# Prompt attention: the threshold search of the long query tiles counts with sign sums on ScalarE, the products for the maxima stand on both sides of the values' products, and the normalisation is done in an earlier slot

## The reference

```python
def indexer_scores(qi, wi, ki, q_pos, k_pos):
    dots = jnp.einsum('bqhd,bsd->bqhs', qi, ki)            # 8 index heads of 64
    s = jnp.einsum('bqhs,bqh->bqs', jax.nn.relu(dots), wi * IDX_SCALE)
    return jnp.where(k_pos[None, None, :] <= q_pos[None, :, None], s, -jnp.inf)
...
    sc = indexer_scores(qib, wib, ki, q_pos, k_pos)
    _, idx = lax.top_k(sc, 256)                             # 256 keys per query
    valid = idx <= q_pos[None, :, None]
    return sparse_attend(qb, gather_rows(k, idx), gather_rows(v, idx), valid)
...
    s = jnp.where(valid[:, :, None, None, :], s, -jnp.inf)  # 16 heads, 4 kv heads of 64
    p = jax.nn.softmax(s, axis=-1)
    o = jnp.einsum('bqngk,bqknd->bqngd', p, v_sel)
```

## Time and profile before

| | |
|---|---|
| median of 3 runs | 6835.29 us (6826.99 to 6841.92) |
| the profiled execution | 6842.18 us |
| its span in the trace | 6840.6 us |
| stretch of the prompt's attention | about 675 to 3090 us of the span |
| busy in that stretch | PE 1783, DVE 1651, ACT 609, POOL 215 us |

### The profile page before, as it was taken

The page is one execution under the profiler, slowest core; times in us unless marked ns, Lnnn a source line. Parts: engine busy times, 40 slices in busy tenths (PEclk is TensorE's granted clock), DMA queues, the critical chain, the costliest instruction groups (busy, mean ns, idle before and its releaser), DMA issues. The chain is left out here.

```text
span 6840.6 us, 60119 instructions
## 1 busy us (share of the span) xinstructions
PE 4944.6 (72%) x16356; PEld 2498.3 (37%) x16408; DVE 2880.7 (42%) x5354; ACT 1429.0 (21%) x2686; POOL 693.7 (10%) x924
## 2 busy tenths in 40 slices
PE   7998466666779888773647569980888887469970
PEld 2443122222223333332113434430665656344430
DVE  1111657778777666630631321104444443331114
ACT  0111212222222223220012212221222322112212
POOL 0112110000000000110022201002000000101012
PEclk9999678888899999985768579995989897579995
DMA  6111000000000000001433477756001000346865
GB/s 232 49 56 60 17 16 11 11 11 7 11 11 8 8 11 18 10 19 25 153 112 117 143 281 275 276 215 216 23 18 37 18 31 11 98 145 248 299 226 175
DMA packets 194804, 634.25 MB, mean 93 GB/s; under 512 B 47033, under 2 KB 65851, under 8 KB 176044
## 3 DMA queue, kind: packets, MB, share of 16 engines
q1 hardware_dynamic: 130318, 412.71, 17.4%
q0 software_dynamic: 38496, 127.70, 5.7%
q10 hardware_dynamic: 25824, 91.88, 3.3%
HBM read 497.48 MB, written 134.79 MB: 92 GB/s over the span
## 5 line engine op out<-in xcount | busy, mean ns | idle before, releaser
L1966 PE MATMUL experts_ps_gu<-w_sb,experts_xT 128*128 x1504 | 681.6, 607 | 36.1 <-DMA w_sb<-moe_w_in 31.7
L815 DVE TENSOR_SCALAR_CACHE_REDUCE attend_passed<-attend_score,attend_cand 128x512 bf16<-128x512 f32 (+13 forms) x448 | 662.6, 1479 | 47.9 <-issue 4.6
L911 PE MATMUL attend_po<-attend_PT,V 128*128 128x512 f32 x1088 | 544.3, 623 | 12.3 <-ACT attend_total L713 12.3
L2475 PE MATMUL recurrent_psAB<-recurrent_hT,rec_w_in_sb 128*128 128x256 f32 (+1 forms) x2304 | 535.0, 392 | 10.6 <-ACT recurrent_hT L2270 10.6
L703 ACT ACTIVATE attend_PT<-attend_big 128x512 f32<-128x512 f32 x544 | 295.4, 595 | 1051.8 <-PE attend_big L900 1051.3
L469 PE MATMUL project_pj<-project_w,project_hT 128*128 128x512 f32 (+2 forms) x1360 | 507.6, 530 | 6.6 <-ACT project_proj L385 5.5
L2475 PEld LDWEIGHTS recurrent_psAB<-recurrent_hT,rec_w_in_sb 128*128 128x128 f32 x2304 | 463.0, 215 | 76.5 <-issue 11.7
L775 DVE TENSOR_REDUCE attend_mx<-attend_aux 128x1 f32<-128x512 f32 (+3 forms) x640 | 365.6, 607 | 187.1 <-PE attend_aux L922 176.2
L1966 PEld LDWEIGHTS experts_ps_gu<-w_sb,experts_xT 128*128 128x128 f32 x1504 | 285.8, 195 | 366.8 <-issue 366.8
L922 PE MATMUL attend_aux<-attend_KTb,attend_qTb 128*128 128x512 bf16 (+3 forms) x640 | 245.2, 388 | 180.9 <-issue 176.6
L933 PE MATMUL attend_aux<-attend_w_out,attend_oT 128*128 128x512 f32 x512 | 258.7, 669 | 155.4 <-DVE attend_oT L789 155.4
(11 more groups left out here) (378 smaller groups left out, 5966.2 us busy)
## 6 DMA issues: line engine op xcount, KB each, us to landing
w_sb<-moe_w_in SPq DMA_DIRECT2D x64, 2048.0 KB, 11.4
w_sb<-moe_w_in SPq DMA_DIRECT2D x64, 1024.0 KB, 8.3
yb_scratch<-experts_y ACTq DMA_DIRECT2D x94, 512.0 KB, 8.2
index_slab<-ada_w_in SPq DMA_DIRECT2D x12, 2048.0 KB, 7.9
sample_V<-cache_v_in POOLq DMA_DIRECT2D x128, 128.0 KB, 2.6
sample_K<-cache_k_in SPq DMA_DIRECT2D x128, 128.0 KB
route_x<-xa_scratch SPq DMA_DIRECT2D x32, 512.0 KB, 4.7
hs_scratch<-route_h ACTq DMA_DIRECT2D x32, 512.0 KB
```

Of the source, the lines that this page charges most:

```text
L815: dve.tensor_scalar(passed[:, 0:L[m]], score[:, m % 2, 0:L[m]], bound, 0.0, op, ALU.add, accum_out=count[:, :])
L911: pe.matmul(po[:, n % 2, :], V1[:, b, n, :], PT[:, g % 4, :], start=(b == 0), stop=(b == S[i] // NKV - 1)).then_inc(pv_done, 1)
L1966: last = pe.matmul(ps_gu[:, u, :], xT[:, u, k, :], w1[:, bass.ds(slot, 1), k, :].rearrange("p a n -> p (a n)"), start=(k == 0), stop=(k == ...
L2475: last = pe.matmul(psAB[:, c % 2, part, 0:W], w_in[:, k, part * D + c * P:part * D + (c + 1) * P], hT[:, k, 0:W], start=(k == 0), stop=(k ...
```

## The change

Four things change, all in `phase_attend`:

1. For the nine tiles with L of at least 1024 (m = 4 to 12, searched in steps 2 to 10), the counts of rounds 1 to 31 are made by ACT: `weigh` sums sign(score + threshold) over the row into `balance`. DVE still makes the count of round 0, asks for the next sum (`asked`), waits for it (`balanced`) and sets the bit. The value in `cand` is kept negated for this.
2. Round 32 of these tiles first works out the threshold from the negated value: ten operations on one column and one more count over the row. Then `finish_search` follows as before.
3. PE does the first half of a slot's `fill`s ahead of `with_values` and the rest behind, in all steps.
4. `normalise` stands in slot 1 (or slot 0 where a step has no other) instead of the middle slot, in all steps.

```diff
+        def by_act(m):
+            return L[m] >= 1024
+        def asked_of(m):
+            return 31 * sum(by_act(k) for k in range(m))
...
+                def weigh(m, r):
+                    act.wait_ge(asked, asked_of(m) + r + 1)
+                    act.activation(passed[:, 0:L[m]], score[:, m % 2, 0:L[m]], ACT.Sign, bias=threshold,
+                                   accum_out=balance[:, :]).then_inc(balanced, 1)
...
                         for pair in pairs_at(i, s):
                             rectify(i + 3, pair)
+                        if there(i + 2) and by_act(i + 2):
+                            for r in share_of(ROUNDS, s, 0, slots(i)):
+                                if r < 31:
+                                    weigh(i + 2, r)
...
+                def search_with_act(m, r):
+                    if r == 0:
+                        counted(m, 0.0, ALU.is_ge)
...
+                        dve.tensor_scalar(cand[:, :], step[:, :], -(1 << 30), None, ALU.bitwise_xor).then_inc(asked, 1)
+                    elif r < 32:
+                        bit = 31 - r
+                        dve.wait_ge(balanced, asked_of(m) + r)
+                        dve.tensor_scalar(step[:, :], balance[:, :], 2 * TOPK - 1.0 - L[m], float(1 << bit), ALU.is_lt, ALU.mult)
+                        dve.drain()
+                        last = dve.scalar_tensor_tensor(cand[:, :], step[:, :], (1 << bit) >> 1, cand[:, :],
+                                                        ALU.bitwise_xor, ALU.bitwise_xor)
+                        if r < 31:
+                            last.then_inc(asked, 1)
+                    else:
...
+                        counted(m, other[:, 0:1].bitcast(F32), ALU.is_ge)
...
+                        finish_search(m)
...
-                        if s == middle(i):
-                            if there(i - 1):
-                                normalise(i - 1)
-                            if there(i + 3):
-                                scale_weights(i + 3)
+                        if s == min(1, middle(i)) and there(i - 1):
+                            normalise(i - 1)
+                        if s == middle(i) and there(i + 3):
+                            scale_weights(i + 3)
...
+                        units = units_at(i, s)
+                        for u in units[:len(units) // 2]:
+                            fill(i + 1, u)
                         if s:
                             with_values(i, 2 * s - 2)
                             with_values(i, 2 * s - 1)
...
-                        for u in units_at(i, s):
+                        for u in units[len(units) // 2:]:
                             fill(i + 1, u)
```

More of the change, by code:

```diff
@@ L516, in phase_attend @@
         cand = sb("cand", [P, 1], I32)
+        balance = sb("balance", [P, 1])
+        other = sb("other", [P, 1], I32)
         passed = sb("passed", [P, SEQ], BF16)
@@ L541, in phase_attend @@
              "y_out", "consts", "spare"))
-        crossed, split_done = sem("crossed"), sem("split_done")
+        crossed, split_done, asked, balanced = (sem(n) for n in ("crossed", "split_done", "asked", "balanced"))
         TILE = [0] + list(range(1, NT, 2)) + list(range(NT - 2, 0, -2))
@@ L591, in all_chosen @@
             return L[m] <= TOPK
+        def by_act(m):
+            return L[m] >= 1024
+        def asked_of(m):
+            return 31 * sum(by_act(k) for k in range(m))
         def rows_of_half(half):
             return slice(half * DH, half * DH + DH)
+        threshold = cand[:, 0:1].bitcast(F32)
         def rows_at(m):
@@ L767, in _ @@
                 dve.wait_ge(consts, 11 + GQ)
-                threshold = cand[:, 0:1].bitcast(F32)
                 def largest(m, u):
@@ L816, in counted @@
                     dve.drain()
+                def search_with_act(m, r):
+                    if r == 0:
+                        counted(m, 0.0, ALU.is_ge)
+                        dve.tensor_scalar(step[:, :], count[:, :], TOPK - 0.5, -1.0, ALU.is_lt, ALU.mult)
+                        dve.drain()
[4 more added lines that the diff above has]
+                        dve.tensor_scalar(step[:, :], balance[:, :], 2 * TOPK - 1.0 - L[m], float(1 << bit), ALU.is_lt, ALU.mult)
+                        dve.drain()
+                        last = dve.scalar_tensor_tensor(cand[:, :], step[:, :], (1 << bit) >> 1, cand[:, :],
[3 more added lines that the diff above has]
+                    else:
+                        dve.drain()
+                        dve.tensor_scalar(cand[:, :], cand[:, :], -(1 << 31), None, ALU.bitwise_xor)
+                        dve.drain()
+                        dve.tensor_scalar(step[:, :], cand[:, :], 23, None, ALU.logical_shift_right)
+                        dve.drain()
+                        dve.tensor_scalar(step[:, :], step[:, :], 0.0, -1.0, ALU.not_equal, ALU.mult)
+                        dve.drain()
+                        dve.tensor_tensor(cand[:, :], cand[:, :], step[:, :], ALU.bitwise_and)
+                        dve.drain()
+                        dve.tensor_scalar(step[:, :], cand[:, :], 31, 1, ALU.arith_shift_right, ALU.bitwise_or)
+                        dve.drain()
+                        dve.tensor_tensor(other[:, :], cand[:, :], step[:, :], ALU.add)
+                        counted(m, other[:, 0:1].bitcast(F32), ALU.is_ge)
+                        dve.tensor_scalar(step[:, :], count[:, :], TOPK - 0.5, -1.0, ALU.is_ge, ALU.mult)
+                        dve.tensor_tensor(other[:, :], other[:, :], cand[:, :], ALU.bitwise_xor)
+                        dve.drain()
+                        dve.tensor_tensor(other[:, :], other[:, :], step[:, :], ALU.bitwise_and)
+                        dve.drain()
+                        dve.tensor_tensor(cand[:, :], cand[:, :], other[:, :], ALU.bitwise_xor)
+                        finish_search(m)
@@ L818, in search @@
                 def search(m, r):
-                    if r == ROUNDS - 1:
+                    if by_act(m):
+                        search_with_act(m, r)
+                    elif r == ROUNDS - 1:
                         finish_search(m)
```

## The result

The changed kernel takes 6792.49 us (median of 4 runs, 6783.89 to 6794.19), the kernel before 6838.6 us beside it (median of 4). The ratio is 0.9935, 95% interval 0.9922 to 0.9948: faster by 0.65%. I had forecast slower by 0.3% (6856 against 6835); the time lies in my range and on the other side of no change.

A forecast was written before the change was run, and what follows sets the result against it. It took PE and DVE to share the attention's bound, with ACT having room. Terms -92 - 9 - 48 + 149 + 11 + 10 = +21 us gave 6863 on the profile's scale, 6856 us on the median's, range 6770 to 6930.

The forecast's parts named there:

- the loop through ACT: Second-half slots with an index-score pair: exponentials, rectifications, `add_up`, ask and sum form a closed chain, 5.7 us against PE's 4.58.
- What bounds it: Attention: PE and DVE share the bound, ACT has room; DVE holds up some first halves, PE bounds second halves.
- First halves: First-half slots: sums on ACT gain 92 us in nine steps, split fills 9 us in steps 11 to 14.
- `normalise`: Middle slots: the wait ahead of the projection goes, -145; its new place in slot 1 costs +97; net -48 us.
- Second halves and tails: Nine steps with sums: closed chain through ACT plus longer tails lose +149 us; the sign rests on this.
- Slot 0: Values' products now behind the wait for `hide`: 1.1 us a step less what the tails hold, +11 us.
- Hand-overs, +10: DVE to ACT in the second halves' sums: 0.1 us each instead of 0.04, +10 us.
- A sum's price: Sign sum on ACT: 0.91 L ns + 0.22 us with the read, 1.73 us at L = 1664; table loads left out.
- The loop does not bind: Rival, second halves: PE's run-ahead hides the chain through ACT, +149 shrinks to 27, 6734 us; chance 0.11.
- First halves shrink to PE's work: Rival: first halves fall to PE's busy time, a further 57 us, 6799 us; chance 0.17.
- The loop also binds the first halves: Rival: late exponentials hold up `with_values` in first halves, the 92 fall to about 30, 6918 us; chance 0.17.
- The change moves nothing: Rival, whole kernel: the halves cancel, 6835 us; chance 0.05.

The follow-up runs named there:

- experiment 4: Kernel before with split fills and `normalise` in slot 1, all counts left on DVE: 6789.01 us, 0.9922.
- experiments 8: Changed kernel with sign sums only in first-half slots and slot 0's values' products ahead of all fills as before: 6693.87 us, 0.98.
- 10: Changed kernel with sums only in first-half slots, slot 0 in its old order, at most two fills ahead of the values' products: 6665.96 us, 0.9764.
- experiment 3: Kernel before with only half of each slot's fills moved ahead of the values' products: 6842.3 us, 1.001.
- 9: Kernel before with only the fills split, at most two of them ahead of the values' products: 6803.2 us, 0.9963.
- experiment 6: Changed kernel with slot 0's values' products ahead of all fills, as before the change: 6761.9 us, 0.9893.
- experiment 7: Changed kernel with ACT's sums only in first-half slots, later rounds counted on DVE: 6713.0 us, 0.983.

## Why the prediction was wrong

The mechanisms and the signs of the terms were right; the forecast fell by two steps in a sum of large terms that cancel. It put the clock of the projection's products behind the wait at nothing, which was worth some 30 us, and it made the loop through ACT too long, which was worth 26 in second halves and tails. Either of them turns +21 into less than zero. Point by point:

- **What bounds it: right in the main.** Over the whole stretch neither PE (74% busy) nor DVE (68%) is near to full; by halves they are. The sums took 11 to 25 us from each first half of steps 3 to 7 (changed kernel against experiment 4) and cost 13 to 20 in their second halves. But the first halves of steps 8 to 10, which I called PE's own work, gained 4.5 to 5.6 us each by the sums too.
- **First halves: right.** Step 6 was to fall to 71.5 + 7.6 = 79.1 us and took 80.0; step 8 to 87.1 - 10 + 6.2 = 83.3, took 81.6 (slots at 4.9, not 5.1); step 3 to 51.5, took 49.9. In all -12 for -4. That is in part luck: `normalise` cost 12 us more than its +97, and sums and split together gave some 20 more than 101. What I missed inside is that half of six `fill`s is three with two buffers. With the sums on ACT that costs less: two at most ahead took 28 us from the first halves between experiments 8 and 10, and 45.6 between 3 and 9. That DVE is then free sooner for the maxima is my explanation of the difference; no run takes it apart.
- **`normalise`: its price near, its gain mis-sized.** +97 for its new place, measured +109 alone. My own terms for the PE-bound steps, 7.8 + 0.5 + 0.9 - 4.3, make 4.9 and not the 6.2 that I took, and steps 7 to 13 paid 6.5 to 9.6: PE's own work hid next to nothing of it. The -145 failed: it was the wait of L933 and nothing else. The row that I quoted, had the other part in it: 671 ns per product at a clock lowered by that very wait. Without the wait it is 603 ns, 13.90 instead of 16.86 us a projection in step 8. Measured -175, 30 us more than forecast: 35 by the products (68 ns less in each of 512), while the wait itself gave 139 of the 145.
- **Second halves and tails: the loop binds, its length mis-sized.** This is the step on which I rested the sign. I forecast 80.0, 112.9 and 97.4 us for step 3, 6 and 8 with their tails, and they took 81.0, 112.9 and 93.6. That steps 3 and 6 fit is luck: to the last `add_up` I had 60.3, 89.3 and 77.0 us and the trace has 58.0, 86.5 and 71.1; from there on I had 19.7, 23.6 and 20.4 and it has 23.0, 26.4 and 22.6. So the loop was too long everywhere and the tails too short everywhere, and where PE binds the two no longer cancelled. In the loop I added up durations that overlap (exponentials to rectifications 0.96 us, not 1.09; 2.15 from the first rectification to the small operations, not 2.24), and the small operations and hand-overs took 0.42, not 0.63: 5.21 us where I had 5.7. And I took every pair as 512 wide, where one in three has 384 keys and its slot took 4.83. PE's slot is 4.57 (4.36 with 384 keys), so the loop exceeds it by about 0.6 and not by 1.1: step 8 lost 9.0 us and not 12.7, only 2.5 of them ahead of its last slot. The agreement with the kernel before on which I trusted the formula (83.7 and 93 for 84.7 and 91.1) was of the same kind, of sums and not of their parts. I also had the neighbour with L = 1920 losing more than step 6; step 7 lost 19.0 and step 6 21.8. Steps 2 to 10 lost 123 for the 149.
- **Slot 0: too small, and hidden.** I took 1.1 us a step. The tails of steps 11 to 13, which have no sums, became 2.8 to 2.9 longer, the split alone lengthened the tails by 32.8 (experiment 3), and the old order gave 24 to 25 back (experiment 6). That the tails without sums come to 12 us together and my whole term to +11 is chance. What I missed is that the values' products run at the low clock after the wait, 3.09 us.
- **Hand-overs, +10: nothing.** The step from the last small operation to the next sum is 0.04 us (2161.19 to 2161.23), as between other engines.
- **A sum's price: right,** 1.68 and 0.19 us that overlap, 1.73 forecast. The Trainium skill (ScalarE: Activation LUTs, What ACT_TABLE_LOAD costs) gives some 280 ns plus 0.833 ns an element for an activation with a pointer as bias, an estimate of 1.67 us at 1664, and the 1681 ns of the row agree; the read of the accumulator, 187 ns, comes on top. The table loads against which the Trainium skill warns (ScalarE: Activation LUTs, Table sets) didn't happen: the trace has no load in the attention, and behind the sums over 1664 elements the exponential starts 1.68 us (median) after the sum.
- **Rivals.** "The loop does not bind" fell (experiment 7). "First halves shrink to PE's work" gave 6799, close to the 6792 measured, by a mechanism that did not occur: step 6's first half took 80.0 us and was to fall below 68 before `normalise`, about 76 with it. "The loop also binds the first halves" fell too: the sums took 110.7 us from them (experiment 4 to the changed kernel). "The change moves nothing" is outside the interval of the ratio.

The 75 us between +21 and -54 are the middle slots, that is the clock behind the wait (30), the second halves and tails of steps 2 to 10 (26, the loop's excess less what the tails lacked), hand-overs (10), and the first halves (8).

## What to carry to other kernels

Work taken off a loaded engine may cost more than it frees when the new place closes a loop: here ask, sum and two small operations run through ACT's in-order queue once a slot, and the move paid only in the first halves, most of all where DVE was the bound (steps 3 to 7). When some of a slot's producers move ahead of other work, no more should move than there are free buffers: with two `aux` buffers the third `fill` was one too many. A wait ahead of a block of matrix products costs its own length and then the lower clock in the products behind it, so a gain that is read as idle time alone is too small; compare the mean of one product in the row with the same product elsewhere.

## What the runs showed of the hardware

- After 8.51 us without work on PE the 32 products of a projection took 16.86 us, with PEclk 0.79 over the first 13.6; right behind other work they took 13.90, at 1.00. With 36 products that nobody reads put into the wait they took 14.00 (0.65 us of wait left), and the program became 0.22% shorter.
- Four values' products took 1.98 us in a full queue, 3.50 behind a wait of 3.64 us, with one `fill` between (granted clock 0.54; such a wait of 3.4 to 3.6 us came in every one of the seven slots), and 3.09 behind one of 15.72 with two `fill`s between.
- In step 4 of experiment 3 a wait in the wrong place and the lower clock came together: the first half went from 58.7 to 80.9 us, PE's busy time from 45.7 to 55.1, its idle time from 13.0 to 25.8, at a granted clock of 0.79 for 0.94. One `fill` less ahead undid both. How much of the idle time would be left at the full clock, no run separates.
